# Modulation vectors of layer 1 summed on VectorE beside the down slabs, each weight piece in two stages

## The chip, the cores and the metric

The program runs on one core of a Trainium2 chip. The metric is device time in microseconds (us) of one execution, from start to end. The kernel before took 3027.91 us, the median of 3 runs (3026.37 to 3031.58).

## The reference

Two blocks follow one another, all in float32, on 256 tokens of width 1024.

The first block has two layers. In each layer two streams (the latent, stream 0, and the context, stream 1) pass through a first feed-forward, a token mixer and a second feed-forward. Each is modulated: nine vectors per layer and stream come from a conditioning vector by one matrix `w_ada` (1024 by 9 x 1024 per layer).

```
m    = silu(c) @ w_ada[l] + b_ada[l]           # nine vectors of 1024: shift, scale, gate, three times
y    = rmsnorm(x, g) * (1 + scale) + shift
x    = x + 0.5 * gate * ((silu(y @ w1) * (y @ w3)) @ w2)     # w1, w3: 1024 x 2816, w2: 2816 x 1024
```

The second block is an attention, convolution and memory mixer and a mixture of 32 experts. The change doesn't touch it.

## The kernel before

**The plan.** `first_order` writes out one list of stages, `plan`, and every engine walks through that same list in order and does its own part of each stage, with semaphores between the engines. So the place of a stage in the list is its place in the order of every engine: TensorE (PE), VectorE (DVE), ScalarE (ACT), GpSimd (POOL) and the queue of SyncE (SP), which issues the weight loads. An engine that waits in one stage holds back all its later ones.

**Slabs.** Weights come as slabs of 128 x 2048 floats (1 MB) into a ring of 5 places; SP loads a slab into a place when the one that was there has been used (L900). A feed-forward of one stream is 22 slabs of gate and up (`gate`, `up`, pairs 0 to 10; one slab gives 256 hidden channels for 256 tokens), then 4 column blocks of the down matrix, each of 22 rows of weights that come in three slabs of `DOWN_K = (8, 7, 7)` rows: 12 down slabs (PE L1276). After the third slab of a block DVE adds the result into the residual (L1919, `x<-ps`), ACT squares it (L1652) and DVE adds the squares up (`h<-h`).

**Halved stages.** For the runs in `HALVED` (layer 0, latent, second feed-forward, pairs 1 to 10, among them) a gate or up slab is made with seven products of half-sized blocks instead of eight (PE L1234: 7 x 4 matmuls of 128 x 128). POOL forms the mixed weights ahead of it (stage `combine`, L2604), ACT copies the first product out of PSUM (L1618), DVE adds the products up in five additions (L1913, `work<-work,ps`), then ACT does the Silu (L1622) or DVE the product with the gate (`work<-work`, 128 x 512). PSUM has four banks for such results (`group`), a halved stage takes two: a stage may only begin when the banks of the stage two before it have been read, and a stage `sum` (one bank, L1295, for the norm) between two of them takes part in that count.

**Modulation vectors.** Some are made on PE (stage `ada`, L1182, four slabs a vector). Others are made on DVE (stage `vada`): a vector has four pieces of `w_ada` of 1 MB each, and DVE multiplies the four quarters of a piece by a scalar each and adds them to a running total: four instructions of 128 x 1024 (L1919, `work<-work,ring`; in the first piece of a vector two of them are L1916). The pieces don't go through the ring but into four buffers `ada_w` of their own; SP issues the load at the place of the stage in the plan, and waits there until the piece four before it has been used (`a_free`, L866). Then PE sums over partitions (`vsum`, L1196), ACT copies the sum (L1611), PE turns it (`turn`, L1207, waits for that copy), and DVE adds the bias.

**Where they lie.** `vector_ada(l, first, last)` makes a list of bundles, one piece in each, with `vsum` two bundles and `turn` three bundles behind the last piece of a vector. `spread_out(main, side, gaps)` lays the bundles evenly between the slabs: bundle i (from 0) of n comes after slab number ceil((i + 1) * gaps / n). In layer 0 the 28 pieces of vectors 2 to 8 lie in the 34 slabs of the first run (context, first feed-forward), whose stages aren't halved. That list also holds `bounds` and `rope` (small tables, on DVE and ACT), the squares and the norm of the latent. The 12 pieces of vectors 2, 3 and 4 of layer 1 (called A, B, C below) lie in the run (0, 0, 1), the latent's second feed-forward of layer 0: 20 bundles over 33 of its 34 slabs, of which the first five hold the last PE-made pieces and `turn`s, so that seven pieces stand among the halved gate and up slabs, the eighth behind the last of these, and four among the down slabs. The context's `sum` and norm for layer 1 is put in the same list, before the gate slab of pair 10.

Of the kernel before, what the change touches and what calls it, by code (L numbers as in the profile page):

```python
# [25 lines left out]
DOWN_K = (8, 7, 7)  # L26
# [24 lines left out]
HALVED = {(0, 0, 1): range(1, 11), (1, 0, 0): range(1, 11), (1, 0, 1): range(2, 11)}  # L51
LENT = 4


def is_halved(stage):

    return stage[0] in ("gate", "up") and stage[4] in HALVED.get(stage[1:4], ())

# [146 lines left out]
def with_halves(plan):  # L205

    before = [[] for _ in plan]
    slabs = [n for n, stage in enumerate(plan) if is_slab(stage)]
    for run in HALVED:
        l, s, j = run  # L210
        mine = [i for i, n in enumerate(slabs) if is_halved(plan[n]) and plan[n][1:4] == run]
        ready = max(n for n in range(slabs[mine[0]]) if plan[n] == ("norm", l, s, 2 * j))
        read = [n for n in range(slabs[mine[0]]) if plan[n][0] == "gmlp"]
        at = max([slabs[mine[0] - 4], ready + 1] + ([read[-1] + 1] if l == 0 and read else []))
        before[at].append(("halves", *run))
        for n, i in enumerate(mine):
            lead = 2 if n < 2 or mine[n - 2] < i - 2 else 1
            before[max(slabs[i - lead], at)].append(("combine", *plan[slabs[i]]))
    return [one for more, stage in zip(before, plan) for one in (*more, stage)]


def places(slabs):

    lent = set()
    for run in HALVED:
        mine = [k for k, stage in enumerate(slabs) if is_halved(stage) and stage[1:4] == run]
        lent |= set(range(mine[0] - 3, mine[-1] + 1))
# [16 lines left out]
def first_order():  # L244
# [104 lines left out]
class Counts:  # L349


    def __init__(self, plan):
# [5 lines left out]
        self.halved, self.halved_slab, self.last_halved, self.halves_at, self.sums_at, self.halved_gates = {}, [], {}, {}, {}, set()  # L358
        self.place, self.lender, self.lent, self.last_in = places([stage for stage in plan if is_slab(stage)])
        for n, stage in enumerate(plan):  # L360
# [9 lines left out]
            if is_halved(stage):  # L370
                assert groups < 4 or self.freed[groups - 4], (n, stage)
                self.freed[groups] = None
                groups += 1
                self.halved[n] = len(self.halved)
                self.halved_slab.append(self.slab[n])
                self.last_halved[stage[1:4]] = self.slab[n]
            if kind == "halves":
                self.halves_at[stage[1:]] = len(self.halves_at)
                self.h_norms[n] = last_norm[stage[2]]
            if kind == "down":  # L380
# [3 lines left out]
                if stage[5] == len(DOWN_K) - 1:  # L384
                    self.d += 1
                    self.freed[self.group[n]] = ("d", self.d)
# [15 lines left out]
            elif is_halved(stage):  # L402
# [4 lines left out]
                if kind == "gate":  # L407
# [3 lines left out]
                    self.halved_gates.add(gates)  # L411
                else:
                    self.d += 1
                    self.up_at[stage[1:]] = self.up_at[gates] = self.d
            elif kind == "gate":
                self.a += 1
                gates += 1
                self.freed[self.group[n]] = ("a", self.a)
                self.gate_at[stage[1:]] = (self.a, gates)
            elif kind == "up":  # L420
                self.d += 1
                self.freed[self.group[n]] = ("d", self.d)
                self.up_at[stage[1:]] = self.up_at[gates] = self.d
            elif kind == "msum":
# [27 lines left out]
            elif kind == "z":  # L452
                self.a += 1
                self.freed[self.group[n]] = ("a", self.a)
                self.z_at[stage[1:]] = self.a
# [8 lines left out]
            elif kind == "vada":  # L464
                self.ada_slab[n] = len(self.ada_slab)
# [15 lines left out]
            if kind in ("gate", "up", "z"):  # L481
                self.h_norms[n] = last_norm[stage[2]]

def build(nc, a, out):
    with ExitStack() as ctx:
# [172 lines left out]
        x_mm = sem("x_mm")  # L660
        one_out = sem("one_out")
# [135 lines left out]
        halves = [shaped(work[:, uv_at + i * 4 * P:uv_at + i * 4 * P + 4 * P], 4, P) for i in range(4)]  # L797

# [12 lines left out]

        def quarters_of_tokens(v):
# [3 lines left out]
        def mixed_of(stage, nth):  # L816

            m = mixed[nth % 2]
            return m[:, :, 0, :], m[:, :, 1, :], mixed4[stage[1:4] in ((0, 1, 0), (1, 1, 0))][nth % 2]
# [23 lines left out]

        units = [("a", s, t) for s in range(4) for t in range(2)] + [("m", s, t) for s in range(4) for t in range(2)]
# [11 lines left out]
        def _(sp):  # L856
            def first():
                for n, stage in enumerate(plan):
                    if stage[0] == "vada":
                        l, i = stage[1:]  # L860
                        k = at.ada_slab[n]
# [262 lines left out]
        def _(pe):  # L1124
# [23 lines left out]
            def first():  # L1148
# [3 lines left out]
                for n, stage in enumerate(plan):  # L1152
# [64 lines left out]
                    elif is_halved(stage):  # L1217
                        g = at.group[n]
                        bx = fresh()
                        if g >= 3:  # L1220
                            pe.wait_ge(*evacuated(g - 3))
                        by = (bx + 1) % 4
                        w, nth = weights(), at.halved[n]
                        h_ready(KD - 1)
                        h_seen = max(h_seen, 8 * at.h_norms[n])
                        (b11, b12), (b21, b22) = quarters_of(w)
                        t3, t2, t4 = mixed_of(stage, nth)
                        s1, s2, s3, s4 = halves
                        (a11, a12), (a21, a22) = quarters_of_tokens(hs[stage[2]])

                        def product(b, place, weight, act):

                            for k in range(4):
                                last = nc.tensor.matmul(ps[:, b, place * P:place * P + P], weight[:, k, :], act[:, k, :],  # L1234
                                                        start=(k == 0), stop=(k == 3), skip_group_check=True)
                            return last

                        product(bx, 2, b11, a11)
                        product(bx, 0, b21, a12)
                        pe.wait_ge(halves_done, at.halves_at[stage[1:4]] + 1)  # L1240
                        product(bx, 1, b22, s4).then_inc(x_mm, 1)
                        pe.wait_ge(combined, nth + 1)
                        product(by, 2, t2, s2)
# [65 lines left out]
                    elif kind == "score":  # L1309
# [16 lines left out]
                        else:  # L1326
                            pe.wait_ge(ev_a, at.z_at[l, s, 7])
# [62 lines left out]
                    elif kind == "cstate":  # L1390
                        hh = stage[1]
                        if hh == 0:
                            pe.wait_ge(ev_a, at.z_at[1, 1, 7])
# [165 lines left out]
        def _(act):  # L1559
# [8 lines left out]
            def first():  # L1568
                for n, stage in enumerate(plan):
# [37 lines left out]
                    elif kind == "vsum":  # L1607
# [4 lines left out]
                                             ACT.Copy).then_inc(ev_a, 1)  # L1612
                    elif is_halved(stage):
                        nth, which = at.gate_at[stage[1:]][1], int(kind == "up")
                        act.wait_ge(x_mm, at.halved[n] + 1)
                        if not which:
                            act.wait_ge(ev_d, at.up_at[nth - 1])
                        nc.scalar.activation(part_sums[:, which, 1, :], ps[:, at.group[n] % 4, 2 * P:3 * P], ACT.Copy  # L1618
                                             ).then_inc(one_out, 1)
                        if not which:  # L1620
                            act.wait_ge(ev_d, at.sums_at[n])
                            nc.scalar.activation(sil[:, 0, :], sil[:, 0, :], ACT.Silu).then_inc(ev_a, 1)  # L1622
                    elif kind == "gate":
                        b = done()
                        nth = at.gate_at[stage[1:]][1]
                        if nth > 2:
                            act.wait_ge(ev_d, at.up_at[nth - (1 if nth - 1 in at.halved_gates else 2)])
# [1144 lines left out]
```

## Time and profile before

| | us |
|---|---|
| median of 3 runs | 3027.91 |
| the profiled execution, its own time | 3027.08 |
| its span, first to last instruction | 3024.9 |
| PE busy | 2844.2 (94%) |
| DVE busy | 1049.0 (35%) |
| ACT busy | 555.6 (18%) |
| POOL busy | 439.4 (15%) |
| DMA, mean over the span | 212 GB/s |

How to read it. In a timeline a row is a start, a length, the engine, the line, the operation with the tiles it writes and reads, how many instructions were merged, and in brackets the idle time before it with what ended it. In a row of windows the numbers are the length of the stretch, the busy time of PE, of PE's weight loads, of DVE, of ACT and of POOL (PE alone where the view was narrowed to it), each with its count of instructions, then the clock that TensorE was granted (1.00 is 2.4 GHz, 0.5 is 1.2 GHz), the busy share of the DMA engines and GB/s. A float32 matmul is two instructions in the records, so a down slab of 8 rows is 32 of them and a halved stage is 56. The run (0, 0, 1) stands between 1046.1 (its first gate matmul) and 1290 us; its halved stages begin at 1060.75, its down slabs at 1209.24.

### The profile page before, as it was taken

What the parts mean: (1) busy time and instruction counts of PE and PEld (TensorE: products, weight loads), DVE (VectorE), ACT (ScalarE), POOL (GpSimd) and SP (SyncE); (2) the same over time, 40 slices, a digit from 0 to 9 for tenths busy, and PEclk for the clock granted to TensorE, in tenths of its full rate; (3) what the DMA queues carried; (4) which work ended last, traced back from release to release, by engine and by line L of the source; (5) the groups of instructions that cost most, each with busy time, mean ns of one, the idle gap of its engine ahead of it and who ended that gap; (6) DMA issues with size and microseconds to landing.
All of it is one profiled execution on the core that took longest, in us unless ns stands there. A gap on an engine that the chain in (4) does not pass through costs nothing.

```text
span 3024.9 us, 39799 instructions
## 1 busy us (share of the span) xinstructions
PE 2844.2 (94%) x17362; PEld 2418.2 (80%) x17362; DVE 1049.0 (35%) x1988; ACT 555.6 (18%) x842; POOL 439.4 (15%) x424
## 2 busy tenths in 40 slices
PE   8999999999999998999999999999999999866666
PEld 6888888888888898889888888889988888533432
DVE  3764034431433348433013433523146412210111
ACT  2101222123211101010023206210012340200000
POOL 0000011200121177058001210028100000000000
PEclk9999999999999999999999999999999999988878
DMA  9775443344333565554544344364433228899998
GB/s 405 272 272 183 151 152 125 127 152 153 139 138 127 195 251 211 186 230 167 168 153 153 134 139 157 129 224 168 167 125 134 103 94 337 367 429 431 429 431 373
DMA packets 74144, 641.47 MB, mean 212 GB/s; under 512 B 8304, under 2 KB 9584, under 8 KB 21232
## 3 DMA queue, kind: packets, MB, share of 16 engines
q1 hardware_dynamic: 71376, 631.55, 55.1%
q10 hardware_dynamic: 2592, 7.33, 0.6%
q8 instruction: 140, 2.29, 0.3%
q14 instruction: 36, 0.29, 0.0%
HBM read 637.80 MB, written 1.05 MB: 211 GB/s over the span
## 4 chain that ended last, share of the span: by engine, by line
PE 82%; DMA 12%; DVE 3%; issue 1%; ACT 1%; POOL 0%; SPq 0%; DVEq 0%; ACTq 0%; POOLq 0%
PE ps L1254 29%; PE ps L1276 18%; DMA ring<-in_w_moe 12%; PE ps L1234 10%; PE ps L1451 7%; PE ps L1264 3%; PE ps L1287 3%; PE ps L1481 2%; PE ps L1055 2%; PE ps L1340 1%; DVE work L1919 1%; DVE work L1913 1%; PE ps L1458 1%; PE ps L1077 1%; DMA ring<-in_w_ada 1%
## 5 line engine op out<-in xcount | busy, mean ns | idle before, releaser
L1254 PE MATMUL ps<-ring 128*128 128x256 f32 x2560 | 560.7, 380 | 0.2 <-ACT ring L1668 0.2
L1254 PEld LDWEIGHTS ps<-ring 128*128 128x128 f32 x2560 | 485.1, 190 | 68.4 <-issue 2.0
L1276 PE MATMUL ps<-work,ring 128*128 128x256 f32 x2464 | 537.9, 379 | 2.0 <-DVE work L1913 2.0
L1276 PEld LDWEIGHTS ps<-work,ring 128*128 128x128 f32 x2464 | 466.1, 190 | 66.5 <-DVE work L1913 2.2
L1254 PE MATMUL ps<-h,ring 128*128 128x256 f32 x1600 | 350.9, 380 | 6.4 <-ACT h L1668 4.2
L1913 DVE TENSOR_TENSOR work<-work,ps 128x128 f32<-128x128 f32 (+3 forms) x414 | 151.2, 400 | 577.0 <-PE ps L1254 292.8
L1254 PEld LDWEIGHTS ps<-h,ring 128*128 128x128 f32 x1600 | 301.0, 190 | 51.7 <-issue 5.6
L2604 POOL TENSOR_TENSOR ring<-ring 128x512 f32<-128x512 f32 x174 | 240.7, 1412 | 367.2 <-DMA ring<-in_w 320.0
L2632 POOL TENSOR_TENSOR work<-work 128x128 f32<-128x128 f32 x168 | 100.2, 635 | 1193.9 <-ACT work L1694 1193.9
L1234 PE MATMUL ps<-work,ring 128*128 128x128 f32 x1856 | 218.0, 276 | 0.5 <-POOL work L2604 0.5
L1234 PEld LDWEIGHTS ps<-work,ring 128*128 128x128 f32 x1856 | 213.2, 193 | 0.7 <-POOL work L2604 0.7
L1913 DVE TENSOR_TENSOR work<-work 128x128 f32<-128x128 f32 (+5 forms) x478 | 192.6, 454 | 50.5 <-ACT eb L1696 24.9
L1451 PE MATMUL ps<-h,ring 128*128 128x256 f32 x928 | 204.9, 379 | 0.5 <-DVE h L1919 0.5
L1451 PEld LDWEIGHTS ps<-h,ring 128*128 128x128 f32 x928 | 174.8, 190 | 27.5 <-issue 4.2
L1919 DVE SCALAR_TENSOR_TENSOR work<-work,ring 128x1024 f32<-128x1024 f32 x140 | 191.8, 1411 | 1.7
L1234 PE MATMUL ps<-h,ring 128*128 128x128 f32 x928 | 117.0, 280 | 9.5 <-DVE work L1913 9.5
L1234 PEld LDWEIGHTS ps<-h,ring 128*128 128x128 f32 x928 | 110.3, 195 | 13.6 <-DVE work L1913 10.8
L1055 PE MATMUL ps<-ring,work 128*32 128x256 f32 x1024 | 72.9, 448 | 37.1 <-DMA ring<-in_w_moe 37.1
L1055 PE MATMUL ps<-work 128*32 128x256 f32 x992 | 72.5, 449 | 34.6 <-DMA work<-in_w_moe 34.0
L1919 DVE SCALAR_TENSOR_TENSOR x<-ps,mod,x 128x256 f32<-128x256 f32 x48 | 21.0, 478 | 228.9 <-PE ps L1276 162.7
L1055 PEld LDWEIGHTS ps<-ring,work 128*32 128x32 f32 x1024 | 40.6, 128 | 68.4 <-issue 56.2
L1055 PEld LDWEIGHTS ps<-work 128*32 128x32 f32 x992 | 40.4, 129 | 65.0 <-issue 52.3
(301 smaller groups left out, 2598.0 us busy)
## 6 DMA issues: line engine op xcount, KB each, us to landing
ring<-in_w SPq DMA_DIRECT2D x182, 1024.0 KB, 4.8
work<-in_w_moe SPq DMA_DIRECT2D x22, 4096.0 KB, 33.8
ring<-in_w_moe SPq DMA_DIRECT2D x22, 4096.0 KB, 33.3
ring<-in_w_in SPq DMA_DIRECT2D x80, 1024.0 KB, 4.8
ring<-in_w SPq DMA_DIRECT2D x56, 896.0 KB, 4.6
work<-in_w_ada SPq DMA_DIRECT2D x40, 1024.0 KB, 6.8
ring<-in_w_ada SPq DMA_DIRECT2D x32, 1024.0 KB, 4.9
ring<-in_w_out SPq DMA_DIRECT2D x16, 1024.0 KB, 4.8
```

The source lines that it names most:

```text
L1055: last = nc.tensor.matmul(ps[i * CAP:i * CAP + CAP, g % 2, 0:256], hg[:, q % 2, k, e * CAP:e * CAP + CAP], w[i][:, k * 256:k * 256 + 256], ...
L1234: last = nc.tensor.matmul(ps[:, b, place * P:place * P + P], weight[:, k, :], act[:, k, :], start=(k == 0), stop=(k == 3), skip_group_chec ...
L1254: last = nc.tensor.matmul(ps[:, b, c * L:c * L + L], w[:, k * L + c * P:k * L + c * P + P], hs[cols][:, k, :], start=(k == 0), stop=(k == ...
L1264: last = nc.tensor.matmul(ps[:, b, t * L:t * L + L], hs[stage[2]][:, k, t * P:t * P + P], w[:, k * L:k * L + L], start=(k == 0), stop=(k = ...
L1276: last = nc.tensor.matmul(ps[:, b, c * L:c * L + L], w[:, k * L + c * P:k * L + c * P + P], hid[:, k0 + k, :], start=(k0 + k == 0 and c == 0),
L1287: last = nc.tensor.matmul(ps[:, b, c * L:c * L + L], w[:, k * L + c * P:k * L + c * P + P], hs[s][:, k, :], start=(k == 0), stop=(k == KD ...
L1451: last = nc.tensor.matmul(ps[:, b, c * L:c * L + L], w[:, k * L + c * P:k * L + c * P + P], hs[0][:, k, :], start=(k == 0), stop=(k == KD ...
L1481: last = nc.tensor.matmul(ps[:, b, c * L:c * L + L], w[:, k * L + c * P:k * L + c * P + P], src[:, k, :], start=(k == 0), stop=(k == kn - 1))
L1913: return nc.vector.tensor_tensor(o, i0, i1, op)
L1919: return nc.vector.scalar_tensor_tensor(o, i0, s, i1, op0, op1)
L2604: return nc.gpsimd.tensor_tensor(o, i0, i1, ALU.subtract)
L2632: nc.gpsimd.tensor_tensor(keys, keys, k_in, ALU.mult)
```

## The change

A piece (`vada`) becomes two stages, c = 0 and c = 1, of two DVE instructions each; the load and its wait stay with c = 0, the release of the buffer with c = 1. In the list of bundles `vsum` stands three and `turn` five of the smaller bundles behind the last one. The companions in layer 0's list keep their relative places (2 becomes 4, and so on). In the run (0, 0, 1) the gate and up slabs keep the five first bundles and the context's `sum` and norm, and all pieces of vectors A, B and C are spread over its 12 down slabs. `DOWN_K` becomes (8, 8, 6) for all feed-forwards. The rest of the diff generalises the halved stages to other kinds of slabs (`z` and `down`); the two tables that would turn these on, `HALVED_Z` and `HALVED_DOWN`, are empty, so `run_of` gives the same stages as before, `halve_hid` returns at once, and the waits of ACT before a gate (`set_free`) name the same or an older event.

```diff
-DOWN_K = (8, 7, 7)
+DOWN_K = (8, 8, 6)
+HALVED_Z = {}
+HALVED_DOWN = []
...
-    out = [[("vada", l, i)] for i in range(4 * first, 4 * last)] + [[], [], []]
+    out = [[("vada", l, i, c)] for i in range(4 * first, 4 * last) for c in range(2)] + [[] for _ in range(5)]
     for i in range(first, last):
-        end = 4 * (i - first) + 3
-        out[end + 2].append(("vsum", l, i))
-        out[end + 3].append(("turn", l, i))
+        end = 8 * (i - first) + 7
+        out[end + 3].append(("vsum", l, i))
+        out[end + 5].append(("turn", l, i))
...
     side = vector_ada(0, 2, 9)
-    side[2] += [("bounds",)]
-    side[4] += [("rope",)]
-    side[6] += [("square", 0, p, "h") for p in range(4)]
-    side[8] += [("sum", 0, "h"), ("norm", 0, 0, 0)]
+    side[4] += [("bounds",)]
+    side[8] += [("rope",)]
+    side[12] += [("square", 0, p, "h") for p in range(4)]
+    side[16] += [("sum", 0, "h"), ("norm", 0, 0, 0)]
...
     run = (0, 0, 1)
-    side = [[("turn", 1, 0)]] + [[stage] for stage in more[5:]] + [[("turn", 1, 1)]] + vector_ada(1, 2, 5)
+    side = [[("turn", 1, 0)]] + [[stage] for stage in more[5:]] + [[("turn", 1, 1)]] + [[] for _ in range(8)]
     side[11] += [("sum", 1, "h"), ("norm", 1, 1, 0)]
-    plan += spread_out(gate_up(run, range(11)) + down(run, range(4)), side, 33)
+    plan += spread_out(gate_up(run, range(11)), side) + spread_out(down(run, range(4)), vector_ada(1, 2, 5))
...
@@ sync
-                    if stage[0] == "vada":
-                        l, i = stage[1:]
+                    if stage[0] == "vada" and stage[3] == 0:
+                        l, i = stage[1:3]
...
@@ vector
-                        for c in range(2):
-                            for r in range(2):
-                                by = cvec[:, 2 * part + c, r:r + 1]
-                                if part == c == 0:
-                                    last = ts(total[:, r, :], w[:, c, :], by, None, mul)
-                                else:
-                                    last = stt(total[:, r, :], w[:, c, :], by, total[:, r, :], mul, add)
-                            if c == 0:
-                                own(last)
-                        last.then_inc(a_free, 1)
-                        dve.wait_ge(a_free, k + 1)
+                        for r in range(2):
+                            by = cvec[:, 2 * part + c, r:r + 1]
+                            if part == c == 0:
+                                last = ts(total[:, r, :], w[:, c, :], by, None, mul)
+                            else:
+                                last = stt(total[:, r, :], w[:, c, :], by, total[:, r, :], mul, add)
+                        if c == 0:
+                            own(last)
+                        else:
+                            last.then_inc(a_free, 1)
+                            dve.wait_ge(a_free, k + 1)
```

## Rows read from the trace of the kernel before

**Rows 1.** The page: busy time of PE.
```profile
PE 2844.2 (94%) x17362; PEld 2418.2 (80%) x17362; DVE 1049.0 (35%) x1988; ACT 555.6 (18%) x842; POOL 439.4 (15%) x424
```

**Rows 2.** Windows of three stretches, all engines.
```profile
1118.00:1209.00 91.00, 79.79 (x674) 77.60 (x672) 81.78 (x102) 13.27 (x28) 71.79 (x42) 0.96 0.60 224
1209.00:1290.00 81.00, 80.76 (x408) 69.54 (x412) 30.75 (x41) 3.77 (x7) 0.00 (x0) 1.00 0.52 184
...
31.00:196.00 165.00, 163.24 (x804) 139.73 (x804) 112.17 (x133) 27.72 (x47) 0.00 (x0) 0.99 0.81 321
```

**Rows 3.** Timeline of PE in the run (0, 0, 1).
```profile
1114.90 1.95 PE L1234 MATMUL ps<-h,ring 128*128 128x128 f32 x16
...
1121.15 1.95 PE L1234 MATMUL ps<-h,ring 128*128 128x128 f32 x16
...
1127.52 2.05 PE L1234 MATMUL ps<-h,ring 128*128 128x128 f32 x16
...
1141.85 2.05 PE L1234 MATMUL ps<-h,ring 128*128 128x128 f32 x16 [1.56 <-DVE work L1913]
...
1156.17 2.05 PE L1234 MATMUL ps<-h,ring 128*128 128x128 f32 x16 [1.54 <-DVE work L1913]
...
1166.35 3.68 PE L1234 MATMUL ps<-h,ring 128*128 128x128 f32 x16 [3.66 <-DVE work L1913]
...
1180.68 1.07 PE L1196 MATMUL ps<-work,ones 128*32 128x256 f32 x16
...
1188.04 0.95 PE L1207 MATMUL ps<-vec,pmt 128*128 128x4 f32 x8
1188.85 1.11 PE L1295 MATMUL ps<-ring,ones 128*128 128x256 f32 x4
1192.66 2.73 PE L1234 MATMUL ps<-h,ring 128*128 128x128 f32 x16 [2.71 <-DVE work L1913]
...
1209.24 19.26 PE L1276 MATMUL ps<-work,ring 128*128 128x256 f32 x88 [1.96 <-DVE work L1913]
...
1292.11 1.10 PE L1295 MATMUL ps<-h,ones 128*128 128x256 f32 x4 [0.58 <-DVE h L1913]
```

**Rows 4.** Windows of PE alone: three stretches behind a stall.
```profile
1166.30:1170.00 3.70, 3.65 (x18) 0.54 0.12 49
1192.60:1200.00 7.40, 7.34 (x51) 0.77 0.27 112
90.00:98.00 8.00, 8.00 (x34) 0.79 0.49 184
```

**Rows 5.** Groups by form, DVE, 1118 to 1200 us: busy us, mean ns.
```profile
L1919 DVE SCALAR_TENSOR_TENSOR work<-work,ring 128x1024 f32<-128x1024 f32 x24 | 48.1, 2042 | 0.2
```

**Rows 6.** The same view, 1209 to 1290 us.
```profile
L1919 DVE SCALAR_TENSOR_TENSOR work<-work,ring 128x1024 f32<-128x1024 f32 x18 | 22.3, 1281 | 0.2
...
L1916 DVE TENSOR_SCALAR work<-work,ring 128x1024 f32<-128x1024 f32 x2 | 1.4, 752 | 0.0
```

**Rows 7.** Timeline of DVE around the end of the halved stages.
```profile
1207.72 1.47 DVE L1913 TENSOR_TENSOR work<-work,ps 128x128 f32<-128x128 f32 x5 [1.99 <-ACT work L1618]
...
1228.60 0.87 DVE L1919 SCALAR_TENSOR_TENSOR x<-ps,mod,x 128x256 f32<-128x256 f32 x2 [7.40 <-issue]
```

**Rows 8.** Timeline of ACT: a copy of a summed vector.
```profile
1276.55 0.60 ACT L1611 ACTIVATE pmt<-ps 128x512 f32<-128x512 f32 x1 [6.34 <-PE ps L1196]
```

**Rows 9.** The page: DMA issues, KB each, us to landing.
```profile
ring<-in_w SPq DMA_DIRECT2D x182, 1024.0 KB, 4.8
```

**Rows 10.** Timeline of PE in the first run.
```profile
89.83 1.05 PE L1207 MATMUL ps<-vec,pmt 128*128 128x4 f32 x8 [1.57 <-ACT pmt L1611]
90.75 15.75 PE L1254 MATMUL ps<-ring 128*128 128x256 f32 x64
```

**Rows 11.** Timeline of ACT in the first run.
```profile
88.08 0.42 ACT L1599 ACTIVATE ring<-ring 128x256 f32<-128x256 f32 x1 [17.56 <-DVE x L1913]
```

**Rows 12.** DMA issue at 25.5 us: KB, us to landing.
```profile
ring<-in_w SPq DMA_DIRECT2D x1, 1024.0 KB, 18.7
```

More of the change, by code:

```diff
@@ L208, in with_halves @@
     slabs = [n for n, stage in enumerate(plan) if is_slab(stage)]
[L209 to L215, printed above, removed]
+    runs = dict.fromkeys(run_of(plan[n]) for n in slabs if is_halved(plan[n]))
+    for run in runs:
+        mine = [i for i, n in enumerate(slabs) if run_of(plan[n]) == run]
+        at = slabs[mine[0] - 4]
+        if run[0] != "down":
+            norm = ("norm", *run[1:], 1) if run[0] == "z" else ("norm", *run[:2], 2 * run[2])
+            ready = max(n for n in range(slabs[mine[0]]) if plan[n] == norm)
+            read = [n for n in range(slabs[mine[0]]) if plan[n][0] == "gmlp"]
+            at = max([at, ready + 1] + ([read[-1] + 1] if run[0] == 0 and read else []))
+            before[at].append(("halves", norm[2], run))
         for n, i in enumerate(mine):
@@ L224, in places @@
     lent = set()
-    for run in HALVED:
-        mine = [k for k, stage in enumerate(slabs) if is_halved(stage) and stage[1:4] == run]
+    for run in dict.fromkeys(run_of(stage) for stage in slabs if is_halved(stage)):
+        mine = [k for k, stage in enumerate(slabs) if run_of(stage) == run]
         lent |= set(range(mine[0] - 3, mine[-1] + 1))
@@ L454, in __init__ @@
                 self.freed[self.group[n]] = ("a", self.a)
[L455 removed]
+                self.z_at[stage[1:]] = ("a", self.a)
             elif kind == "wo":
@@ L1217, in first @@
                     elif is_halved(stage):
[L1218 to L1221, printed above, removed]
+                        g, piece, run = at.group[n], 0, run_of(stage)
+                        if kind == "down":
+                            piece = stage[5]
+                        bx = g % 4
                         by = (bx + 1) % 4
+                        if piece == 0:
+                            fresh()
+                            if g >= 3:
+                                pe.wait_ge(*evacuated(g - 3))
@@ L1223, in first @@
                         w, nth = weights(), at.halved[n]
-                        h_ready(KD - 1)
-                        h_seen = max(h_seen, 8 * at.h_norms[n])
-                        (b11, b12), (b21, b22) = quarters_of(w)
+                        (b11, b12), (b21, b22) = weights_of(stage, w)
                         t3, t2, t4 = mixed_of(stage, nth)
[L1228 to L1235, printed above, removed]
+                        tokens_first = kind == "z" and stage[3] in (4, 5, 6, 7)
@@ new lines, in first @@
+                        if kind == "down":
+                            k0 = sum(DOWN_K[:piece]) // 2
+                            ks = slice(k0, k0 + DOWN_K[piece] // 2)
+                            up = ("up", *stage[1:4], ks.stop - 1)
+                            pe.wait_ge(ev_d, at.up_at[up[1:]])
+                            pe.wait_ge(hid_halved, at.hid_halves[up[1:]])
+                            s1, s2, s3, s4 = (one[:, ks, :] for one in hid_sums)
+                            (a11, a12), (a21, a22) = ([hid_of[:, ks, e, t * P:t * P + P] for e in range(2)] for t in range(2))
+                        else:
+                            h_ready(KD - 1)
+                            h_seen = max(h_seen, 8 * at.h_norms[n])
+                            s1, s2, s3, s4 = z_halves if kind == "z" else halves
+                            (a11, a12), (a21, a22) = quarters_of_tokens(hs[stage[2]])
@@ new lines, in product @@
+                        def product(b, place, weight, act, first=False):
+                            many = weight.shape[1]
+                            for k in range(many):
+                                one, other = weight[:, k, :], act[:, k, :]
+                                last = nc.tensor.matmul(ps[:, b, place * P:place * P + P], *((other, one) if tokens_first else (one, other)),
+                                                        start=(k == 0 and (first or kind != "down")),
+                                                        stop=(k == many - 1 and sums_follow(stage)), skip_group_check=True)
```

233 lines of the change are left out of this document (173 added, 60 removed).

## The prediction

> **What bounds the kernel now.** I read the page first: PE is busy for 94% of the span [rows 1], so a gain has to be idle time of PE, or time at a lower clock. Then the windows of the stretches that the diff touches [rows 2]. In the first run of layer 0 PE is busy for 163.2 of 165 us. In the run (0, 0, 1) it is busy for 80.8 of 81 us in the down slabs, but for only 79.8 of 91 us in the second half of the halved slabs, where DVE is busy for 81.8 and POOL for 71.8 us and the clock is 0.96. Beside the down slabs DVE does 31 us of 81 and POOL nothing. So VectorE is full in one half of this run and nearly empty in the other.
>
> The timeline of PE puts a name to the idle time [rows 3]: stalls of 1.56, 1.54, 3.66, 2.71 and 1.96 us, all released by additions of DVE, 11.4 us together. Halved stages without a stall start 6.25 and 6.37 us apart (1114.90, 1121.15, 1127.52), 6.31 on average. From 1121.15 to the down slabs at 1209.24 there are 11 of them, 69.4 us, with a `vsum` (1.0), a `turn` (0.8) and a `sum` (1.0): 72.2 us of work in 88.1. The excess is 15.9 us: 11.4 idle, and 4.5 in which PE worked slowly. That is mostly the clock: it was granted at 0.54 for 3.7 us behind the longest stall and at 0.77 for 7.4 us behind the one of 2.71 [rows 4], so partly at its lower level of 1.2 GHz: 1.7 us lost in each.
>
> Why DVE is late is in the groups by form: the instruction of a piece, 128 x 1024, takes 2042 ns on average while POOL mixes weights [rows 5] and 1281 ns beside the down slabs, with POOL idle [rows 6]. A piece of four is 8.2 us against 5.1. A halved stage lasts 6.3, so additions that stand behind a whole piece come late, and PSUM has no bank for PE.
>
> **The pieces of layer 1 leave the halved slabs.** What stays there for DVE is five additions (1.5 us) a stage and a product of 0.7 (at most 1.5 beside POOL) every second one: some 2.2 of 6.3 us. POOL mixes for 5 us a stage when alone. The rows of PE at 1114.90 to 1127.52 have no idle time before them [rows 3], and there the first pieces had only begun. I take the whole excess as gone: -15.9. Its bounds are 11.4 (the idle time alone) and 15.9.
>
> New there: the context's `sum` now stands between gate 10 and up 10. With its one bank in the count, up 10 needs the banks of gate 10 itself. DVE reads these within 1.5 us of gate 10's end, and the `sum` covers 1.0: a wait of some 0.6 us (0 to 2.7, the stall at the same kind of place before). The wait of 1.96 at the first down slab had this `sum` behind it too: the norm on ACT held back the copy for gate 10, so its additions began at 1207.72 [rows 7]. Now that norm stands behind gate 10, and the first down slab needs only gate 10's banks. Late instead is up 10, whose product the third down slab wants 14 us on.
>
> **The same pieces beside the down slabs.** In them are 42 instructions of 1.281 us and 6 of 0.752 [rows 6], 58.3 us in all: 2.6 us a half piece, 1.5 the first of a vector. With the residual (0.9) and an addition of squares (0.7) for each of four blocks and small ones, DVE has some 66 us of work in 81. Whether PE waits depends on the order, so I walk it, T counted from the first down slab. A block takes 19.3 us [rows 3], its slabs 7.0, 7.0 and 5.3. Half piece i comes behind slab ceil((i + 1) x 12 / 29); `vsum` of A, B, C stands behind slabs 5, 8, 12, their `turn` behind 6, 9, 12.
>
> DVE is through with up 10 at T = 3.5 (the norm of the context on ACT ends at about 1, then a copy, the additions, the product). Halves 0 to 3 end at 12.7. DVE waits for block 0 until 19.3, residual to 20.2, halves 4 to 6 to 27.9, squares 28.6, half 7 to 31.2. PE wants it for `vsum` A at 33.3: 2.1 us in hand. Halves 8 to 11 to 40.4 (block 1 ended at 39.5, its residual is done at 41.3, and no bank is short); 12 and 13 with a bias 46.8, squares 47.5, 14 and 15 to 52.6. PE wants them at 54.3: 1.7 in hand. 16 to 18 to 59.2, block 2's residual at 61.5, then all the rest with its squares until 75.4; PE wants it at 80.7. So there is no wait but one: C's `turn` follows its `vsum` with no slab between, and needs ACT's copy of 0.60 us [rows 8]: 0.7 us. In turn the 0.58 us before the latent's `sum` at 1292.11 [rows 3] go, since two ada slabs and the `turn` lie before it. A's `vsum` and `turn` (1.8) only move from one half to the other. Net +0.1, between 0 and +4 if both narrow margins are missed by 2 us.
>
> SP issues in order, so a ring slab behind a piece now also waits for the piece four before it. The worst is down slab 9, behind piece 9, which waits for piece 5 (half 11, T = 40.4). PE wants that slab at 55, and a slab lands 4.8 us after its issue [rows 9]. Nothing is late.
>
> **Layer 0.** Here PE has one stall: 1.57 us before the `turn` of vector 2, released by ACT's copy [rows 10]. ACT was late because it sat 17.6 us in `rope`, waiting for DVE, until 88.08 [rows 11]. Before `rope` DVE now has 4.5 pieces instead of 5, and only a half one, not a whole one, between up 2 and `rope`; `bounds` lies a stage earlier. `rope` should start 2.5 us or more sooner, ACT's copy then ends before 88.3, where PE would be ready. The stall had a second price: in the 8 us behind it the clock was 0.79 [rows 4], 1.7 us. Together -3.3 (0 to -3.3). `vsum`s and `turn`s keep their slabs but for one `turn`, a slab earlier, whose copy is ready.
>
> Against it: four loads of pieces are issued one slab earlier, so up 0, gate 1, up 1 and gate 2 have 1 MB more before them in a queue that is full. 28 pieces in 34 slabs keep the DMA at 0.81 and 321 GB/s on average [rows 2]; at full share that would be about 400 GB/s, so 1 MB is 2.6 us. Up 1 landed 18.7 us after 25.5 [rows 12], at 44.2, and is wanted after three slabs, at 52. At 46.8 it is still in time. The Trainium skill says in "DMA: Bandwidth & Descriptors", Queues, rings and completion order, that each DMA engine takes turns between the queue rows it has work for. ACT's constants load then as well, so by that rule an added MB could cost twice its time, 5.2 us, and up 1 would land at 49.4: no loss either. The trace gives only the sum of both queues here and can't decide it.
>
> **DOWN_K.** The same bytes and matmuls. The third slab starts two rows (four matmuls, 0.9 us) later and wants the same product, for which PE waits nowhere now: 0, within 0.5 us either way. The two stages of a piece keep the same waits within DVE: 0. The generalised halved stages are empty: 0.
>
> **Sum.** -15.9 + 0.6 + 0.1 - 3.3 = -18.5 us. The profiled execution took 3027.1 us (its span 3024.9, with 2.2 outside), so 3008.6 for one like it. That is 0.8 below the median of the runs, so I predict a median of 3009.4. The expert stage at the end starts from what was loaded before, so what is saved early I take as saved at the end.
>
> **The clock's part.** I count 4.5 and 1.7 us of slow work as going with the stalls [rows 3, 4]. The skill says in "TensorE: Matmul & The Clock Gate", What's actually happening, that the moment of the change depends on where in a free-running window the work falls, and varies between runs. By that rule the clock's share in this one profile need not be that of the median, and the sum would lie between -18.5 and -12.3. Two stalls of 1.5 us and one of 1.96 in rows 3 show no slow stretch behind them, one of 1.57 does [rows 10]: the trace agrees that like stalls don't cost alike.
>
> **Rivals.** (1) *The idle time goes, the slow work doesn't, or the margins of 2 us at the `vsum`s are missed.* -12.3, or -18.5 + 4: about 3015. For it: margins of 1.7 and 2.1 us rest on a schedule added up, and new stalls would carry new slow stretches. Against it: DVE idles for 6 us before block 0's end, which takes up a late start. Chance 0.15. (2) *The stall changes places.* DVE at the `vsum`s is 4 us later than I think, at each of them, and layer 0 gains nothing: -15.2 + 8, 3021 to 3024. Chance 0.05. (3) *Slower.* Pieces are slow not because of POOL but because their buffers are being loaded, and beside the down slabs, with 12 MB more to load in 80 us, they stay at 2.04 us. Then the pieces are 42 x 2.04 + 6 x 1.2 = 93 us, with 3.5 at the start and 7.3 of other work 104, and PE, ready for `vsum` C at 80.7, waits 23 us: +4.5, about 3032. It begins to cost at 1.56 us an instruction and eats the gain at 2.0. Against it: 1281 ns at 184 GB/s [rows 2, 6], and DVE's 112 us in layer 0 at 321 GB/s [rows 2] leave no stall. Chance 0.03.
>
> **Chances and range.** The forecast has 0.77. 0.2% (6 us) is about what a measurement of this kernel tells from no change. Faster: the forecast, rival 1 and part of 2, 0.92; within 0.2%: 0.05; slower: 0.03. The range takes in rival 1 and its lower end a few more us of slow work saved: 3004 to 3018.
>
> **What would show it.** Right: no idle before halved stages released by DVE work; the 128 x 1024 group at about 1280 ns on average over all 140, POOL's mixes near 1300; the first down slab about 145 to 148 us behind the first gate matmul (163.1 now: 1046.1 to 1209.24); 85 us from there to the latent's `sum` (82.9 now); no stall at the `turn` of vector 2. Wrong: PE idle before L1196 on DVE, released by L1919; a half piece over 1.5 us an instruction; PE waiting for a ring slab in the first run; a clock below 1.00 in the new run.

## The result: 0.67% faster, where it was forecast

| | before | changed |
|---|---|---|
| median in this comparison (4 runs each) | 3029.61 us | 3008.86 us |
| lowest to highest | 3026.37 to 3031.58 | 3007.53 to 3011.58 |
| own time of the profiled execution | 3027.08 us | 3009.36 us |
| its span | 3024.9 us | 3007.5 us |

The ratio is 0.9933, with a 95% interval of 0.9922 to 0.9945. The forecast was 3009.4, with a range of 3004 to 3018. In two later comparisons the changed kernel was 16.1 and 19.8 us faster than before by the medians.

The stretch where the time was, in windows of the changed kernel (columns as in [rows 2]): the halved slabs from where the pieces stood before, then the down slabs.
```profile
1118.00:1188.00 70.00, 69.19 (x616) 68.76 (x615) 27.82 (x70) 11.19 (x24) 52.07 (x40) 1.00 0.60 217
1188.00:1273.00 85.00, 84.28 (x461) 71.84 (x460) 64.30 (x73) 5.48 (x11) 0.00 (x0) 1.00 0.69 267
```
Against [rows 2] DVE fell from 82 busy us in 91 to 28 in 70, and beside the down slabs rose from 31 in 81 to 64 in 85. (Of the 21 us between 91 and 70, some 3.5 are only that the run starts earlier now.) PE lost 0.8 and 0.7 us in them, and the clock is 1.00 in both.

The timeline of PE in the same run, with every row between 1042 and 1290 us that has idle time before it, the first down slab and the `vsum`s of A and B.
```profile
1042.67 14.40 PE L1364 MATMUL ps<-h,ring 128*128 128x256 f32 x64 [1.27 <-ACT h L1784]
...
1182.05 2.02 PE L1340 MATMUL ps<-h,ring 128*128 128x128 f32 x16 [0.81 <-DVE work L2029]
...
1188.37 32.97 PE L1386 MATMUL ps<-work,ring 128*128 128x256 f32 x152
1221.27 1.07 PE L1286 MATMUL ps<-work,ones 128*32 128x256 f32 x16
...
1242.36 1.07 PE L1286 MATMUL ps<-work,ones 128*32 128x256 f32 x16
...
1268.62 1.07 PE L1286 MATMUL ps<-work,ones 128*32 128x256 f32 x16
1270.41 1.05 PE L1297 MATMUL ps<-vec,pmt 128*128 128x4 f32 x8 [0.72 <-ACT pmt L1721]
1271.40 1.93 PE L1272 MATMUL ps<-ring 128*32 128x256 f32 x32
1273.26 1.13 PE L1405 MATMUL ps<-h,ones 128*128 128x256 f32 x4
...
1278.39 7.50 PE L1364 MATMUL ps<-h,ring 128*128 128x256 f32 x32 [1.27 <-ACT h L1784]
```
The five stalls of [rows 3] are gone. In their place stand the two that the change makes, 0.81 and 0.72 us. From the first gate matmul to the first down slab it is 145.7 us (163.1 before), from there to the latent's `sum` 84.9 (82.9).

DVE in the down slabs, from its timeline:
```profile
1189.31 1.47 DVE L2029 TENSOR_TENSOR work<-work,ps 128x128 f32<-128x128 f32 x5 [1.99 <-ACT work L1732]
1190.88 0.69 DVE L2029 TENSOR_TENSOR work<-work 128x512 f32<-128x512 f32 x1
1191.49 1.42 DVE L2032 TENSOR_SCALAR work<-work,ring 128x1024 f32<-128x1024 f32 x2
1192.94 7.51 DVE L2035 SCALAR_TENSOR_TENSOR work<-work,ring 128x1024 f32<-128x1024 f32 x6
1207.62 0.88 DVE L2035 SCALAR_TENSOR_TENSOR x<-ps,mod,x 128x256 f32<-128x256 f32 x2 [7.17 <-issue]
1208.42 10.02 DVE L2035 SCALAR_TENSOR_TENSOR work<-work,ring 128x1024 f32<-128x1024 f32 x8
...
1234.59 4.99 DVE L2035 SCALAR_TENSOR_TENSOR work<-work,ring 128x1024 f32<-128x1024 f32 x4
...
1255.47 7.51 DVE L2035 SCALAR_TENSOR_TENSOR work<-work,ring 128x1024 f32<-128x1024 f32 x6
```
Less 1188.37 these are the T of the walk. The pieces begin at 3.1 (forecast 3.5), half 7 ends at 30.1 (31.2), half 15 at 51.2 (52.6), the last at 74.6 (75.4), and PE takes the `vsum`s at 32.9, 54.0 and 80.3. Between halves 4 and 7 there is no addition of squares: `h<-h` stands three times in this stretch, not four times as in the walk, and never for block 0. The page's group of these instructions, and POOL's mixes:
```profile
L2760 POOL TENSOR_TENSOR ring<-ring 128x512 f32<-128x512 f32 x174 | 227.7, 1337 | 368.9 <-DMA ring<-in_w 315.7
...
L2035 DVE SCALAR_TENSOR_TENSOR work<-work,ring 128x1024 f32<-128x1024 f32 x140 | 173.5, 1281 | 1.6
```
The first run of layer 0, PE, where [rows 10] had the stall of 1.57 and a slow stretch:
```profile
88.14 0.95 PE L1297 MATMUL ps<-vec,pmt 128*128 128x4 f32 x8
88.95 14.06 PE L1364 MATMUL ps<-ring 128*128 128x256 f32 x64
```
ACT left `rope` at 84.52 there (88.08 before), and its copy of the sum ends at 86.2, before PE wants it at 88.1.

What was saved up to the latent's `sum` is 18.85 us (1292.11 to 1273.26). The span is only 17.4 shorter. One loss in between is plain in the rows: at 1878.97 PE does slowly what the kernel before did at speed, behind the same stall of 2.16 us.
```profile
1878.97 8.86 PE L1364 MATMUL ps<-h,ring 128*128 128x256 f32 x32 [2.16 <-DVE rs L2032]
```
In the kernel before:
```profile
1897.99 7.17 PE L1254 MATMUL ps<-h,ring 128*128 128x256 f32 x32 [2.16 <-DVE rs L1916]
```
The granted clock in the 9 us from these starts is 0.81 in the changed kernel and 1.00 in the one before. What was saved early did carry over to the end: PE waits 131.8 us in all for loads of the expert stage (tiles of `in_w_moe`), for 133.4 before.

### The profile page after: what moved, and what is told of

It is laid out like the page before. It is cut to its first block, busy times and chain, and to the rows that moved or that the text cites. A ratio compares the mean times of both kernels' runs of the same rounds, so it can differ in the third digit from the quotient of the medians.

```text
span 3007.5 us, 39866 instructions
## 1 busy us (share of the span) xinstructions
PE 2840.7 (94%) x17362; PEld 2414.2 (80%) x17362; DVE 1027.7 (34%) x1988; ACT 553.7 (18%) x840; POOL 422.0 (14%) x424
## 3 DMA queue, kind: packets, MB, share of 16 engines
q8 instruction: 140, 2.29, 0.3%
## 4 chain that ended last, share of the span: by engine, by line
PE 86%; DMA 13%; DVE 1%; issue 0%; ACT 0%; POOL 0%; SPq 0%; DVEq 0%; POOLq 0%; ACTq 0%
PE ps L1364 30%; PE ps L1386 18%; PE ps L1340 12%; DMA ring<-in_w_moe 12%; PE ps L1561 7%; PE ps L1374 3%; PE ps L1397 3%; PE ps L1591 2%; PE ps L1145 2%; PE ps L1450 1%; DMA ring<-in_w_ada 1%; PE ps L1568 1%; PE ps L1167 1%; PE ps L1536 0%; PE ps L1539 0%; PE ps L1272 0%
## 5 line engine op out<-in xcount | busy, mean ns | idle before, releaser
L2760 POOL TENSOR_TENSOR ring<-ring 128x512 f32<-128x512 f32 x174 | 227.7, 1337 | 368.9 <-DMA ring<-in_w 315.7
L2035 DVE SCALAR_TENSOR_TENSOR work<-work,ring 128x1024 f32<-128x1024 f32 x140 | 173.5, 1281 | 1.6
L1145 PEld LDWEIGHTS ps<-work 128*32 128x32 f32 x992 | 39.2, 126 | 66.2 <-issue 52.6
```

Source lines behind the costliest of these rows:

```text
L1145: last = nc.tensor.matmul(ps[i * CAP:i * CAP + CAP, g % 2, 0:256], hg[:, q % 2, k, e * CAP:e * CAP + CAP], w[i][:, k * 256:k * 256 + 256], ...
L2035: return nc.vector.scalar_tensor_tensor(o, i0, s, i1, op0, op1)
L2760: return nc.gpsimd.tensor_tensor(o, i0, i1, ALU.subtract)
```

## The experiments

The theory: beside POOL's mixes a piece takes DVE so long that the halved slabs have more DVE work than time; moving the pieces is what pays in that run, splitting them only in layer 0. The rival: PE waited for additions that stood behind a whole piece, and the split is what pays.

**Moved whole.** The kernel before with one edit.
```diff
-    side = [[("turn", 1, 0)]] + ... + [[("turn", 1, 1)]] + vector_ada(1, 2, 5)
+    side = [[("turn", 1, 0)]] + ... + [[("turn", 1, 1)]] + [[] for _ in range(8)]
-    plan += spread_out(gate_up(run, range(11)) + down(run, range(4)), side, 33)
+    plan += spread_out(gate_up(run, range(11)), side) + spread_out(down(run, range(4)), vector_ada(1, 2, 5))
```


> The kernel before with one thing changed: the 12 pieces of layer 1's vectors A, B and C, whole, lie in the 12 down slabs of the run (0, 0, 1); no piece is split, DOWN_K stays (8, 7, 7). Theory (the halved slabs had more work for DVE than time, because a piece runs at 8.2 us beside POOL and 5.1 without it; moving is what pays there, splitting pays only in layer 0): the run is as short as in the changed kernel, 145.7 us from the first gate matmul to the first down slab, and no wait at the vsums, since even whole pieces end at T = 31 and 52 of 33 and 54; layer 0 keeps its stall of 1.57 us and the slow stretch behind it. 15.2 us faster than before, ratio 0.995. Rival (whole pieces block the residual and the squares beside the down slabs, the split is needed there): PE waits at L1196 for DVE, 3 us or more, and the gain is under 12 us.

Measured 3013.31 us, ratio 0.9948 (0.9932 to 0.9965), 16.5 us faster for 15.2 expected. Its PE rows in the run:
```profile
1046.92 14.05 PE L1254 MATMUL ps<-h,ring 128*128 128x256 f32 x64 [2.01 <-DMA ring<-in_w]
1185.93 2.02 PE L1234 MATMUL ps<-h,ring 128*128 128x128 f32 x16 [0.81 <-DVE work L1913]
...
1192.26 32.11 PE L1276 MATMUL ps<-work,ring 128*128 128x256 f32 x148
1224.30 1.07 PE L1196 MATMUL ps<-work,ones 128*32 128x256 f32 x16
```
145.3 us to the down slabs, no wait at a `vsum`, and layer 0 keeps its stall (1.58) and the 15.74 us for the 64 matmuls behind it. So the split does nothing measurable in this run. The wait of 2.01 us for a ring slab was not expected; it is taken up below.

**Split only.** The changed kernel with the pieces back at their old places, in halves.
```diff
-    side = [[("turn", 1, 0)]] + [[stage] for stage in more[5:]] + [[("turn", 1, 1)]] + [[] for _ in range(8)]
-    side[11] += [("sum", 1, "h"), ("norm", 1, 1, 0)]
-    plan += spread_out(gate_up(run, range(11)), side) + spread_out(down(run, range(4)), vector_ada(1, 2, 5))
+    side = [bundle for stage in [("turn", 1, 0), *more[5:], ("turn", 1, 1)] for bundle in ([stage], [])] + vector_ada(1, 2, 5)
+    side[22] += [("sum", 1, "h"), ("norm", 1, 1, 0)]
+    plan += spread_out(gate_up(run, range(11)) + down(run, range(4)), side, 33)
```


> The changed kernel with the pieces of vectors A, B and C back among the halved slabs, at the places of before, but split in two stages each; layer 0 and DOWN_K as changed. Theory (too much work): DVE had 82 us of work in a stretch in which PE has 72, so splitting alone moves the additions forward by at most 4 us each and the work not at all; the excess of the run stays at 10 to 16 us (15.9 before), and only layer 0's 3.3 us and up to 5 are gained: 3 to 8 us faster than before, ratio 0.9974 to 0.999. Rival (blocking: an addition behind a whole piece of 8.2 us is what PE waited for, behind 4.1 it is in time): the excess falls below 4 us, and this is 15 us or more faster than before.

Measured 3020.02 us, ratio 0.9969 (0.9958 to 0.9981), 9.8 us faster, a little more than expected. The run takes 158.2 us to the down slabs, so its excess is 11.0 (163.1 less 15.9, or 147.2, is the run without any). Some of its PE rows:
```profile
1042.63 7.50 PE L1364 MATMUL ps<-h,ring 128*128 128x256 f32 x32 [1.27 <-ACT h L1784]
...
1155.33 2.94 PE L1340 MATMUL ps<-work,ring 128*128 128x128 f32 x24 [1.35 <-POOL work L2760]
...
1185.08 3.75 PE L1340 MATMUL ps<-h,ring 128*128 128x128 f32 x16 [2.69 <-DVE work L2029]
...
1200.83 19.26 PE L1386 MATMUL ps<-work,ring 128*128 128x256 f32 x88 [0.39 <-DVE work L2029]
```
and DVE's group between 1110 and 1200 us:
```profile
L2035 DVE SCALAR_TENSOR_TENSOR work<-work,ring 128x1024 f32<-128x1024 f32 x22 | 48.2, 2230 | 0.1
```
With DVE less in the way PE comes to the next resource, POOL's mixes, slowed just as DVE is: four waits on POOL of 0.17 to 1.35 us, which I had not foreseen. Two engines are short there, and of the two edits only the move relieves both.

**POOL taken off.** The kernel before; from the third halved stage of the run on POOL mixes only 8 columns of one row of each block. This leaves most of the mixing out, so the mixed weights of that run are mostly stale.
```diff
+                    if nth >= 2 and stage[2:5] == (0, 0, 1):
+                        t3, t2, t4, b11, b12, b21, b22 = (one[:, 0:1, 0:8] for one in (t3, t2, t4, b11, b12, b21, b22))
                     minus(t3, b12, b22).then_inc(pool_own, 1)
```


> The kernel before, but in the run (0, 0, 1) POOL mixes only 8 columns of one row of each weight block from the third halved stage on, so the mixed weights of that run are mostly stale: this leaves out mixing, to take POOL off. The pieces stay where they were, whole. Read in the run alone. Theory (contention with POOL makes the work too much): an instruction of a piece falls from 2.04 to 1.28 us, DVE needs 2.2 + 3.1 = 5.3 us of a stage's 6.3, and the excess of the run falls from 15.9 to 2 to 5 us (the wait of 1.96 behind the context's norm stays). Rival (the loads or the number of instructions slow DVE, not POOL): 2.04 us and the excess stay as they are.

Measured 3018.01 us (one run; only its run (0, 0, 1) is read, since work is left out): the instruction of a piece falls to the price that it has beside the down slabs.
```profile
L1919 DVE SCALAR_TENSOR_TENSOR work<-work,ring 128x1024 f32<-128x1024 f32 x25 | 31.0, 1281 | 0.2
```
```profile
1045.43 15.74 PE L1254 MATMUL ps<-h,ring 128*128 128x256 f32 x64 [2.03 <-DMA ring<-in_w]
...
1196.08 20.95 PE L1276 MATMUL ps<-work,ring 128*128 128x256 f32 x88 [1.96 <-DVE work L1913]
```
To the first down slab it is 150.65 us, an excess of 3.4: in the main the wait of 1.96 behind the context's norm and 1.7 of slow work at the run's start. All other stalls are gone with the pieces where they were. So POOL's mixing is the cause, not the count of instructions on either engine.

**POOL put on.** The changed kernel with 40 subtractions of 128 x 512 on POOL, from the first down slab on.
```diff
+                if stage == ("down", 0, 0, 1, 0, 0):
+                    pool.wait_ge(fb_slab, at.last_halved[0, 0, 1] + 1)
+                    for _ in range(40):
+                        minus(kvs[:, 0:4, :], kvs[:, 4:8, :], kvs[:, 4:8, :]).then_inc(pool_own, 1)
+                        pool.wait_ge(pool_own, S.next(pool_own))
```


> The changed kernel with POOL kept busy beside the down slabs of the run (0, 0, 1): 40 subtractions of 128 x 512 on a scratch area, from the first down slab on. The result stays right. Theory (POOL is what makes a piece slow, and my walk through DVE's order is right): an instruction of a piece takes 2.0 to 2.3 us while POOL works, some 80 of the 85 us; PE, ready for vsum A at T = 33.3, waits 6 to 10 us for the half piece 7, and the stretch from the first down slab to the latent's sum grows from 84.9 to 105 to 113 us. Rival (a piece was slow in the halved slabs for its loads or its place, not for POOL): 1.28 us, 84.9 us, no wait at L1286.

Measured 3028.72 us (one run), beside medians of 3011.51 for the changed kernel and 3027.62 for the one before: the whole gain is lost. PE waits at the `vsum`s, as the walk says it must when a half piece is late:
```profile
1224.45 1.07 PE L1286 MATMUL ps<-work,ones 128*32 128x256 f32 x16 [2.87 <-DVE work L2035]
1225.45 7.13 PE L1386 MATMUL ps<-work,ring 128*128 128x256 f32 x24
...
1256.75 1.93 PE L1286 MATMUL ps<-work,ones 128*32 128x256 f32 x16 [9.46 <-DVE work L2035]
1258.62 7.62 PE L1386 MATMUL ps<-work,ring 128*128 128x256 f32 x24
```
The stretch to the latent's `sum` grew to 102.1 us, 17.2 more: 12.3 of idle time and 4.8 of slow work behind it. I had expected 6 to 10 us where it waited 2.87, and 105 to 113 for the 102.1.
```profile
L2760 POOL TENSOR_TENSOR work<-work 128x512 f32<-128x512 f32 x40 | 68.6, 1714 | 12.0 <-PE ps L1340 8.9
```
POOL was busy for 68.6 us, not 80, and the mean instruction of a piece took 1745 ns. Even while POOL worked six of them in a row took 11.84 us, 1.97 each, less than the 2.29 that the slowest took beside the mixing in the kernel before. The mechanism held, the size was over-estimated.

**The rows of the down slabs.** `DOWN_K = (8, 7, 7)` in the changed kernel, twice, and (8, 8, 6) as the only edit of the kernel before.

> The changed kernel with DOWN_K = (8, 7, 7) as before. Theory: no effect, PE waits for no product of the last pair and for no down slab in either kernel; within 1 us of the changed kernel, 19 to 20 us faster than before, ratio 0.9933. Rival: the smaller third slab matters (0.9 us more cover for the last product, 28 loads of 768 KB instead of 56 of 896): slower than the changed kernel by 0.9 us or more in each run that waits, with PE idle before the down matmuls.

> The changed kernel with DOWN_K = (8, 7, 7) again. Four of five profiles of kernels with (8, 7, 7) have PE waiting for a ring slab at the first gate of the run (0, 0, 1) (1.56 to 2.30 us in place of 1.27 for ACT's norm), none of five with (8, 8, 6). Theory (the rows matter there): it shows the wait again, and is 0.3 to 1 us slower than the changed kernel. Rival (landing times of that slab vary, its margin is near zero in every kernel): either way, and the time within the noise.

> The kernel before with DOWN_K = (8, 8, 6) and nothing else. Theory of no effect: ratio 1.000 within its interval, the six stalls of before at their sizes. Rival (the rows matter for the ring): no wait for a ring slab at the first gate of the run (0, 0, 1), which one of two profiles of before shows (2.30 us, with a slow stretch of 1.3 behind it), and up to 1 us faster than before.

Measured 3009.32 us (ratio 0.9937, 0.9921 to 0.9954) and 3010.67 (0.9937, 0.9923 to 0.9951), where the changed kernel had 3008.86 (in another comparison) and 3009.03 (in the same); and for the last 3027.79, ratio 0.9999 (0.999 to 1.0008), with the stalls of before at their sizes. No effect that can be told from the spread. In the second run with (8, 7, 7) the wait that I expected didn't come; its median is 1.6 us above the changed kernel's beside it, but the runs overlap (3008.44 to 3011.55 and 3007.88 to 3011.09). PE waits at the first gate of the run for a ring slab in four of six profiles with (8, 7, 7) (1.56 to 2.30 us in place of 1.27 for ACT), and in none of eight with (8, 8, 6). The same kernel shows it in one profile and not in the next, both for the changed one with (8, 7, 7) and for the kernel before, so the rows don't decide it alone; whether they shift the odds stays open.

**The two new waits.** The changed kernel with the context's `sum` and norm behind the first down slab, and C's `turn` behind the next ada slab; run twice.
```diff
-    side[11] += [("sum", 1, "h"), ("norm", 1, 1, 0)]
-    plan += spread_out(gate_up(run, range(11)), side) + spread_out(down(run, range(4)), vector_ada(1, 2, 5))
+    plan += spread_out(gate_up(run, range(11)), side)
+    side = vector_ada(1, 2, 5)
+    side[1] += [("sum", 1, "h"), ("norm", 1, 1, 0)]
+    side[28].remove(("turn", 1, 4))
+    plan += spread_out(down(run, range(4)), side)
-    plan += more[:2] + [("sum", 0, "h"), ("inv", 0)] + more[2:5] + [("norm", 1, 0, 0)]
+    plan += more[:1] + [("turn", 1, 4)] + more[1:2] + [("sum", 0, "h"), ("inv", 0)] + more[2:5] + [("norm", 1, 0, 0)]
```


> The changed kernel with its two new waits taken away: the context's sum and norm stand behind the first down slab instead of between gate 10 and up 10, and C's turn stands behind the next ada slab instead of directly behind its vsum. Theory (both waits are bare idle time with something else to put there): the 0.81 us before up 10 and the 0.72 us before that turn go, DVE does the norm in the 7 us in which it idled before block 0, the run takes 143.9 us to the first down slab (145.7 less 0.8 and less the sum's 1.0), the down stretch to the latent's sum 85.2 (84.9 plus 1.0 less 0.7): 1.5 us faster than the changed kernel, ratio to before 0.9930. Rival (the norm's 5 us make DVE late beside the down slabs, where the margins at the vsums were 2 us): PE waits at L1286 for DVE, and the 1.5 us are given back or more.

> The kernel with the late norm again, to see whether its 1.5 us stand out of the noise of one chip. The first time its run (0, 0, 1) was 1.8 us shorter in the trace up to the latent's sum, and its median 1.0 us lower than the changed kernel's. Theory: 1.5 to 2 us faster than the changed kernel in this job too. Rival (what is saved there is lost in the spread of slow stretches and of the expert stage's loads): within 1 us of it, or slower.

Measured 3010.54 us (ratio 0.9937, 0.9923 to 0.9950), beside 3011.51 of the changed kernel on the same chip, and 3006.30 (0.9927, 0.9913 to 0.9940) beside 3009.03. Over the ten runs of each in these two comparisons the medians are 3008.4 and 3010.5. In the second profile the run has two rows with idle time, neither of them new:
```profile
1042.78 14.41 PE L1367 MATMUL ps<-h,ring 128*128 128x256 f32 x64 [1.27 <-ACT h L1787]
1276.66 7.51 PE L1367 MATMUL ps<-h,ring 128*128 128x256 f32 x32 [1.27 <-ACT h L1787]
```
233.9 us from one to the other, 235.7 in the changed kernel beside it: 1.8 us for 1.5 expected; the two medians differ by 2.1. DVE's slack before block 0 took the norm. It is the fastest version here, though by the intervals of the ratios alone it can't be told from the changed one.

**The same kernels again.** For a second and third profile.

> The changed kernel once more, beside the one with the late norm, for a second profile and more runs. Theory (which slow stretches of TensorE follow a stall is chance, each worth about 1.7 us): the stalls are the same to 0.1 us, the slow stretch behind the stall of 2.16 us near 1879 may be there or not, and the time lies within 1.7 us of 3009.4 for each such stretch more or less. Rival (the slow stretches belong to the kernel): the same ones in the same places.

> The changed kernel a third time, as the partner of the others. Chance theory: the slow stretch of 1.7 us behind the stall of 2.16 us near 1879, which 6 of 10 profiles show so far whatever the kernel, may be there or not; all other stalls before the expert stage the same.

> The kernel before once more, for a second profile. Theory (chance): its five stalls in the run (0, 0, 1) and the one of 1.57 us in the first run come again at the same sizes, while the slow stretches behind them (0.54 behind 3.66 us, 0.77 behind 2.71, 0.79 behind 1.57, none behind 2.16) change places. Rival: the same stretches again.

Measured 3011.51 us (ratio 0.9939, 0.9925 to 0.9952), 3009.03 (0.9936, 0.9922 to 0.9949), and 3035.74 for the one run of the kernel before. Its stalls came again at 1.55, 1.56, 3.65 and 2.70 us, the one before the first down slab at 1.25 for 1.96, and the one in layer 0 at 1.56. The slow stretches did in part. Behind 3.66 and 2.70 us PE was slow in all three profiles of kernels with the pieces in the old places unsplit and POOL at work, behind the two stalls of about 1.55 in none of them. Behind the stall of 1.57 in layer 0 it was slow in four of five, by 1.7 us in three, and twice that in one:
```profile
91.16 17.02 PE L1254 MATMUL ps<-ring 128*128 128x256 f32 x64
```
Behind the same stall of 2.16 us PE needs 8.86 (once 8.79) us in six of 14 profiles and 7.17 in eight. The changed kernel has it slow in two of three, so both the chance theory and its rival were half right: stalls of 2.7 us and more always cost it here, those of 1.57 to 2.3 sometimes.

## Why the prediction was right

- *The stalls, -15.9, and the `sum` between gate 10 and up 10, +0.6.* With A's `vsum` and `turn` leaving (1.8) I had -17.1 to the first down slab; it was -17.4. The whole excess went, slow work too, as rows at full speed show. The new wait was 0.81 us.
- *DVE beside the down slabs, +0.1 net.* I had nearly every point of the walk late, by up to 1.5 us. From half 7 on, 0.7 of that is the addition of squares that I had counted for block 0 and that isn't there. The margins at the `vsum`s were 2.8 us for 2.1 and 1.7. The stretch to the latent's `sum` grew by 2.0 for 1.9, C's `turn` waited 0.72 for 0.7, the 0.58 before the `sum` went. The price of 1.281 us stood although the DMA now moves 267 GB/s there: rival 3 is refuted by that row. (It spoke of 12 MB more. Four of the twelve pieces were loaded there before: 81 us at 184 GB/s and 85 us at 267 are 14.9 and 22.7 MB, 7.8 more.) Its arithmetic (too slow pieces end in a wait at a `vsum`) is confirmed by the experiment with POOL put on.
- *Layer 0, -3.3.* The run (0, 0, 1) begins 3.5 us earlier, and ACT leaves `rope` 3.6 us sooner (I had 2.5 or more). In the split-only kernel the stall is gone too and in the moved-whole one it stays, so it is the split list that does it; the half pieces and the slightly earlier place of `bounds` came together and weren't tried apart.
- *The clock's share.* I took it as going in full and named the other sum, -12.3. In the stretch it did go: -18.85 measured for -18.5. But 1.7 of it was given back at 1878.97, so the profiled pair differs by 17.7. The medians differ by 20.75, 16.1 and 19.8 in three comparisons; 18.5 lies among them. Single totals don't say more about the clock's share than that. That the median 3008.86 came within 0.6 us of 3009.4 is partly luck: with a fourth run the kernel before stood at 3029.61 and no longer at 3027.91, so the difference was 2.2 us larger than forecast.
- *DOWN_K and the generalised stages, 0.* The rows are within the noise, by three kernels. The generalised stages were not tried alone; PE, DVE and POOL run the same number of instructions as before (17362, 1988, 424), and the stretches above leave nothing over for them.
- *The ring behind the pieces, nothing late.* SP waited 44.9 us for pieces in the down slabs, and PE for no ring slab there. The wait at the run's first gate, in other kernels, I had not looked at: its load is issued 6.5 us before PE wants it and has next to no margin.

## What to carry to other kernels

Before making an engine's instructions faster, see what runs beside them: the same VectorE work cost 2.0 to 2.3 us in one place and 1.28 in the next, and it slowed GpSimd as well. A list that all engines walk through can be checked for such a move: add up the busy engine's durations in order, and compare with when the others want each result; the two narrow margins came out 0.7 and 1.1 us wider than forecast here. And a stall of TensorE is worth more than its idle time, often by 1.7 us here and up to twice that, but not each time, so compare stretches in the trace and not single totals.

## What the runs showed of the hardware

- VectorE instructions of 128 x 1024 with two inputs in SBUF (`work<-work,ring`) took 1281 ns alone. Beside GpSimd's mixing they took 2042 (before) and 2230 ns (split only) on average, and 2286 in the median of the twelve between 1121 and 1158 us, while GpSimd's instructions of 128 x 512 went from 1337 ns, their average in the changed kernel, to 1770. The one-input multiplications of 128 x 1024 went from 752 to 1595 ns. Additions of 128 x 128 with one input in PSUM took 285 ns in both. From the kernel before:
```profile
L1919 DVE SCALAR_TENSOR_TENSOR work<-work,ring x12: 2133/2286/2289, 1121.6 to 1158.1; 128x1024 f32<-128x1024 f32 x12
...
L2604 POOL TENSOR_TENSOR ring<-ring 128x512 f32<-128x512 f32 x31 | 54.0, 1770 | 4.4 <-PE ps L1234 4.4
```
  The Trainium skill, "GPSIMD Engine Reference", Specifications, names contention with VectorE instructions of two SBUF inputs. The trace agrees, and the price is the one above.
- The move raised the loads beside these instructions from 184 to 267 GB/s (14.9 to 22.7 MB in the two stretches) and left them at 1281 ns.
- A stall of 2.16 us at the same place had a slow stretch of 1.7 us behind it in six of 14 profiles. Two stalls of about 1.55 us had none in three profiles, one of 1.57 had it in four of five.
